# The last round of an expert loop written out, and the rounding of the next weights moved

## What is computed

```
# moe_ffn, after the router chose two experts of 16 per token
h = silu(einsum('td,edf->tef', xt, w_gate)) * einsum('td,edf->tef', xt, w_up)
h = h * comb[:, :, None]                       # gates of the chosen experts
return einsum('tef,efd->td', h, w_down)        # D = 1024, F = 512
...
# then, between the layers
x = layer_norm(DEEPNORM_ALPHA * x + ffn, ln2_g[l], ln2_b[l])
k, v = split(x @ kv_w); q = x @ w_q            # layer 1's projections
```

## Time and profile before

| | |
|---|---|
| median of 3 runs | 696.32 us (696.08 to 697.30) |
| the profiled execution | 695.99 us |
| its span, first to last instruction | 694.2 us |
| mean granted TensorE clock | 0.997 |
| PE busy | 683.0 us (98%) |
| DVE busy | 307.3 us (44%) |
| ACT busy | 229.5 us (33%) |
| POOL busy | 56.4 us (8%) |
| DMA, mean over the span | 352 GB/s |

### The profile page before, as it was taken

One profiled execution on the slowest core, in us unless ns is written; L12 is line 12 of the kernel. 1 busy time (PEld: TensorE's weight loads), 2 busy tenths in 40 slices (PEclk: granted clock), 3 DMA queues, 4 the chain that ended last, 5 costly groups with the idle time before them and its releaser, 6 DMA issues.

```text
span 694.2 us, 13450 instructions
## 1 busy us (share of the span) xinstructions
PE 683.0 (98%) x5516; PEld 408.4 (59%) x5517; DVE 307.3 (44%) x561; ACT 229.5 (33%) x432; POOL 56.4 (8%) x58
## 2 busy tenths in 40 slices
PE   9999999999999999999999999999999999999994
PEld 8989988864335335335379987887433533533531
DVE  5689956687111112112067677778711111111214
ACT  4566567152111112112173656716211111211211
POOL 2025100010000000000025000001000000000001
PEclk9999999999999999999999999999999999999998
DMA  8999334989999999999999743498999999999991
GB/s 311 311 373 397 139 121 182 406 336 423 398 422 422 419 422 419 409 422 419 415 386 390 272 157 124 180 389 343 414 414 422 421 411 422 419 406 421 421 414 68
DMA packets 51030, 244.04 MB, mean 352 GB/s; under 512 B 6233, under 2 KB 6450, under 8 KB 26418
## 3 DMA queue, kind: packets, MB, share of 16 engines
q1 hardware_dynamic: 50994, 243.55, 87.7%
HBM read 242.49 MB, written 1.05 MB: 351 GB/s over the span
## 4 chain that ended last, share of the span: by engine, by line
PE 91%; DVE 7%; issue 1%; ACT 1%; DVEq 0%; ACTq 0%
PE ps L2200 32%; PE ps L1960 11%; PE ps L1955 9%; PE ps L2214 8%; PE ps L2231 8%; PE ps L2181 5%; PE ps L2162 4%; DVE ring_lo L1214 2%; PE ps L1922 2%; PE ps L2170 1%; PE ps L1873 1%; PE ps L2128 1%; PE ps L2268 1%; PE ps L1895 1%; PE ps L1980 1%
## 5 line engine op out<-in xcount | busy, mean ns | idle before, releaser
L2200 PE MATMUL ps<-weights,scratch 128*32 128x512 f32 (+1 forms) x1536 | 167.8, 592 | 0.1
L2200 PEld LDWEIGHTS ps<-weights,scratch 128*32 128x32 f32 x1536 | 49.9, 110 | 114.0 <-issue 114.0
L1214 DVE TENSOR_TENSOR ring_lo<-weights,w_hi 128x2048 fp32r<-128x2048 f32 x35 | 83.1, 2392 | 9.2 <-ACT w_hi L818 9.0
L1730 DVE TENSOR_TENSOR scratch<-ps,early 128x512 f32<-128x512 f32 x16 | 11.0, 690 | 168.1 <-PE ps L2200 168.1
L818 ACT ACTIVATE w_hi<-weights 128x2048 fp32r<-128x2048 f32 x34 | 64.8, 1913 | 23.4 <-PE ps L1960 11.5
L1711 DVE SCALAR_TENSOR_TENSOR rounded<-ps,gslot,rounded 128x512 fp32r<-128x512 f32 x30 | 22.5, 751 | 86.3 <-ACT rounded L1080 86.3
L2200 PE MATMUL ps<-tail,scratch 128*32 128x512 f32 (+1 forms) x512 | 56.4, 592 | 0.0
L1040 ACT ACTIVATE scratch<-ps,ln_col 128x256 f32<-128x256 f32 (+1 forms) x40 | 19.4, 541 | 86.9 <-PE ps L2181 84.6
L1080 ACT ACTIVATE rounded<-ps,gslot 128x512 fp32r<-128x512 f32 x30 | 20.6, 688 | 82.9 <-PE ps L2231 41.5
L1058 ACT ACTIVATE early<-ps 128x512 f32<-128x512 f32 x16 | 9.6, 598 | 98.8 <-PE ps L2200 98.8
L2200 PEld LDWEIGHTS ps<-tail,scratch 128*32 128x32 f32 x512 | 16.6, 110 | 38.3 <-issue 38.3
(11 more groups left out here) (304 smaller groups left out, 1006.7 us busy)
## 6 DMA issues: line engine op xcount, KB each, us to landing
weights<-in_moe_w_gate SPq DMA_DIRECT2D x64, 1024.0 KB, 13.4
weights<-in_moe_w_up SPq DMA_DIRECT2D x32, 1024.0 KB, 11.7
places<-in_moe_w_down SPq DMA_DIRECT2D x32, 1024.0 KB, 11.8
tail<-in_moe_w_up SPq DMA_DIRECT2D x32, 1024.0 KB, 17.6
weights<-in_moe_w_down SPq DMA_DIRECT2D x32, 1024.0 KB, 11.8
weights<-in_a_w_in SPq DMA_DIRECT2D x15, 1024.0 KB, 12.7
weights<-in_kv_w SPq DMA_DIRECT2D x8, 1024.0 KB, 15.4
weights<-in_a_w_out SPq DMA_DIRECT2D x4, 1024.0 KB, 15.2
```

What stands on the lines that cost most here:

```text
L1214: V.tensor_tensor(low_part(i), ring[:, piece_slot(i), :, :], w_hi[:, i % HI, :, :].bitcast(F32), ALU.subtract).then_inc(lo_ready, 1)
L2200: last = mm(ps[rows, bank, :], own[:, HALF_K * part + k, rows], w, start=part == 0 and k == 0, stop=part == 1 and k == HALF_K - 1)
```

## The change

- The loop on PE runs three rounds, and the fourth is written out behind it. There `gather` has 128 moving columns, for the one pair that is left, and ACT and DVE take 128 columns out of PSUM; `add_up` is no longer behind a branch; and the odd pair's down projection goes part by part.
- ACT rounds piece 20 where it rounded piece 21, behind both evictions, and piece 21 behind its share of rounded and whole x.
- POOL no longer makes the rest of piece 20. DVE does, between the rests of the two halves of x. Piece 20 has the products in the order 0, 1, 2.
- The fill on zeros is 14 matmuls of 128 columns and 74 of 64, where there were 40 and 29.

```diff
+        def gathered_columns(two):
+            return slice(0, 2 * SLOTS if isinstance(two, int) and two == PAIRS // 2 - 1 else 4 * SLOTS)
...
                 weigh(PAIRS // 2 - 1, 1)
                 if layer == 0:
-                    i = A_PIECES
-                    pool.wait_ge(hi_ready, i + 1)
-                    pool.tensor_tensor(low_part(i), ring[:, piece_slot(i), :, :], w_hi[:, i % HI, :, :].bitcast(F32),
-                                       ALU.subtract).then_inc(lo_ready, 1)
...
-                        take_xe(xe_ps, gathered(layer, two, 0) + 1, BANK_C, (0, 1), slice(0, 4 * SLOTS))
+                        take_xe(xe_ps, gathered(layer, two, 0) + 1, BANK_C, (0, 1), gathered_columns(two))
...
                         nc.scalar.activation(rows, ps[:, bank, :], ACT.Copy, scale=gslot[:, 0:1]).then_inc(ys_act, 1)
-                        if last_pair and part == layer == 0:
-                            high(A_PIECES)
...
                 overflow()
                 if layer == 0:
-                    high(A_PIECES + 1)
+                    high(A_PIECES)
...
             rounded_and_whole(0)
             rounded_and_whole(1)
+            high(A_PIECES + 1)
...
                 V.tensor_tensor(x_lo[:, ks, :], xT[:, ks, :], x_hi[:, ks, :].bitcast(F32), ALU.subtract
                                 ).then_inc(x_lo_ready, 1)
-                if half == 1:
-                    dve.wait_ge(lo_ready, A_PIECES + 1)
-                    low(A_PIECES + 1)
+                low(A_PIECES + half)
...
-                for number in (0, 2, 1) if i == A_PIECES else range(3):
-                    w, xs = products[number]
+                for number, (w, xs) in enumerate(products):
...
-                def gather(ks, banks):
+                def gather(ks, banks, pairs=2):
+                    width = pairs * 2 * SLOTS
                     for j, k in enumerate(ks):
-                        first = (j % 2) * 4 * SLOTS
+                        first = (j % 2) * width
...
-                            last = mm(ps[:, banks[j // 2], first:first + 4 * SLOTS], part[:, t, k * P:(k + 1) * P],
-                                      pick[:, t, :, :].rearrange("p e s -> p (e s)"), start=n == 0, stop=n == 3)
+                            last = mm(ps[:, banks[j // 2], first:first + width], part[:, t, k * P:(k + 1) * P],
+                                      pick[:, t, 0:4 * pairs, :].rearrange("p e s -> p (e s)"), start=n == 0, stop=n == 3)
...
-                def experts(two, odd):
+                def experts(two, odd, last_pairs=False):
+                    pairs = 1 if last_pairs else 2
...
                     if odd:
                         add_up(1)
+                    elif last_pairs:
+                        add_up(0)
+                        add_up(1)
                     else:
                         with pe.If(two > 0):
...
-                    if odd:
+                    if odd and last_pairs:
+                        pe.wait_ge(ht_ready, pair + 1)
+                        out_of_hidden(two, odd, 0, who)
+                        out_of_hidden(two, odd, 1, who)
+                    elif odd:
                         pe.wait_ge(ht_ready, pair + 1)
                         out_by_banks(two, odd, who)
...
-                with pe.Fori(0, PAIRS // 2, 1) as two:
+                with pe.Fori(0, PAIRS // 2 - 1, 1) as two:
                     experts(two, 0)
                     experts(two, 1)
+                experts(PAIRS // 2 - 1, 0, last_pairs=True)
+                experts(PAIRS // 2 - 1, 1, last_pairs=True)
...
-            for _ in range(40):
+            for _ in range(14):
                 nothing(BANK_A, COLS // 4)
-            for _ in range(29):
+            for _ in range(74):
                 mm(ps[:, BANK_A, 0:SLOTS], zeros16[:, :], zeros16[:, 0:SLOTS], start=True, stop=True)
```

More of the change, by code:

```diff
@@ L1066, in experts @@
                     if not odd:
-                        take_xe(xe_ps, gathered(layer, two, 0) + 2, BANK_B, (4, 5), slice(0, 4 * SLOTS))
+                        take_xe(xe_ps, gathered(layer, two, 0) + 2, BANK_B, (4, 5), gathered_columns(two))
                     act.wait_ge(put_ps, pair + 2)
@@ L1732, in experts @@
                     if not odd:
-                        take_xe(gathered(layer, two, 0) + 1, (2, 3), slice(0, 4 * SLOTS))
+                        take_xe(gathered(layer, two, 0) + 1, (2, 3), gathered_columns(two))
                     if not odd:
-                        take_xe(gathered(layer, two, 0) + 2, (6, 7), slice(0, 4 * SLOTS))
+                        take_xe(gathered(layer, two, 0) + 2, (6, 7), gathered_columns(two))
                     dve.wait_ge(gslot_ready, pair + 1)
@@ L2260, in experts @@
                         pe.wait_ge(xr_ready, 2 * layer + 2)
-                        gather(range(0, 4), (BANK_C, BANK_D)).then_inc(xe_ps, 1)
+                        gather(range(0, 4), (BANK_C, BANK_D), pairs).then_inc(xe_ps, 1)
                     if odd:
@@ L2277, in experts @@
                     if not odd:
-                        gather(range(4, 6), (BANK_B,))
+                        gather(range(4, 6), (BANK_B,), pairs)
                         pe.wait_ge(xe_dve, gathered(layer, two, 0) + 1)
-                        gather(range(6, 8), (BANK_D,)).then_inc(xe_ps, 1)
+                        gather(range(6, 8), (BANK_D,), pairs).then_inc(xe_ps, 1)
                         pe.wait_ge(ht_ready, pair + 1)
```

## The result

| | before | changed |
|---|---|---|
| median in the same job | 696.07 us (695.84 to 697.30, 6 runs) | 700.06 us (698.82 to 700.74, 6 runs) |
| profiled execution | 695.99 us | 700.42 us |
| span | 694.2 us | 698.5 us |
| mean granted TensorE clock | 0.997 | 0.995 |

The ratio is 1.0054, with a 95% interval of 1.0044 to 1.0064: the change makes the kernel slower by about 4 us, outside the predicted range, and I had given slower a chance of 0.14. Of the six executions two kept a mean granted clock of 0.997 and took 698.82 and 699.22 us; the other four, at 0.993 to 0.995, took 699.99 to 700.74.

What follows compares the result with a forecast made beforehand. The prediction took PE, busy for 98% of the span, as the bound; gather's -0.5 us and the moved rounding's +0.5 summed to 0.0 on 695.99, a median of 696.3 us, with a range of 694.8 to 697.9.

Steps and rivals of the forecast that it cites:

- Step 2: Narrower evictions on ACT and DVE, the branch around add_up and the loop's end: nobody waits, so 0.
- Step 6: The fill: 2.9 us in place of 3.1, either ending before DVE's x is there, so 0.
- the third rival: The thin fill lets TensorE's clock fall before pieces 20 and 21: 2.2 us, 698.5 us; chance 0.05.
- Step 1: Gather's 64 narrow matmuls in the last rounds: step from 0.119 to 0.112 us, limited by weight loads, -0.5 us.
- both ends of the bound: Gather's narrow step as low as 0.056 us, like bf16 (-4.0 us), or 0.22, like true float32 (+6.6 us).
- Step 3: Last down chunks part by part: eviction margin 0.08 us, cost 0; late chunk's margin of 0.25 us widens, gain 0.
- Step 4: ACT's rounding of pieces 20 and 21 between the layers: done before PE reaches piece 21, so 0.
- Step 5: Rest of piece 20 moved from POOL to DVE: two PE waits, 0.27 and 0.24 us, together +0.5 us, in layer 0.

Runs made afterwards that it cites:

- Run 10: Kernel before with the last round written out in both layers and its gather at 128 columns, nothing else changed: 700.35 us, ratio 1.0054.
- run 9: Changed kernel with TensorE's jumped-over overflow code left out for layer 0: 695.98 us, ratio 0.9993 to the kernel before.
- run 2: Kernel before with only the new thin fill, 14 matmuls of 128 columns and 74 of 64: 696.62 us, ratio 1.0007.
- run 1: Changed kernel with the fill of before, 40 matmuls of 128 columns and 29 of 64: 698.63 us, ratio 1.0037 to the kernel before.
- run 11: Kernel before with the last round written out and gather at 128 columns in layer 1 alone, down projection bank by bank: 696.29 us, ratio 0.9999.
- run 12: Kernel before with layer 1's last round alone written out, narrow gather, and its odd pair's down projection part by part: 695.85 us, ratio 0.9999.
- run 7: Kernel before with only the moved rounding on ACT, DVE and POOL and piece 20's order 0, 1, 2: 697.75 us, ratio 1.0012.
- run 5: Changed kernel with a never-taken branch of 64 matmuls at the start of PE's program: 700.83 us, in two groups; ratio 1.0057 to the kernel before.

## Why the prediction was wrong

- **Step 2 failed:** "the cover is the work that PE has already queued." It put leaving the loop at 0, and a gap of 2.81 us was there. The instruction queue carried no packet between 192 and 352 us before, and four in the changed kernel: the loop's rounds run on code that is at hand, a written-out round brings its own. With it the block boundary and the jump over the overflow code fell so that 54 matmuls were left when PE needed the next block. Run 10 shows that the written-out round is enough for the gap, and run 9 that the gap goes with the overflow code; how the jump and the place of the boundary share in it stays open. I looked for the gap at the start of the written-out round; it came behind its end, where the matmuls are shortest.
- **Step 6 failed with it:** "Either ends before DVE's x is there at 357.79, so 0." True where instructions are there (runs 2 and 9). In the change the time from the fill's start to the transposes grew by 2.95 us. I compared lengths, and did not ask whether a shorter matmul uses up code faster: 54 matmuls cover 1.95 us with the new fill, 2.64 with the old one (run 1).
- **The clock** did fall, as the third rival said, and cost 1.09 us on the transposes and some 0.7 on the fill, which the 2.95 contain. But it fell behind the gap, not because of the thin fill: run 2 has the thin fill, no gap and no loss of clock. It need not fall: behind the gap of run 10 it stayed up.
- **Step 1 was right.** 16 narrow steps take 1.74 us, 0.109 each, where I took 0.112; both ends of the bound, -4.0 and +6.6, are out. Two layers gain 0.17 x 4 = 0.7 us in the groups, 0.3 per layer over the whole stretch.
- **Step 3 was right in cost, too small in worth.** C's rest ended before PE read it, and no wait stood there. But the margin of 0.25 us was not enough once `gather` was quicker: run 11 has the wait of 0.78 us, run 12 does not. In run 11 PE came to the chunk some 0.3 us earlier than before, and the chunk landed at 677.24, 0.6 us later than before; why it took longer, 18.4 us where it took 17.4, is not shown. I gave the order no gain since nothing waited; with the round written out something would.
- **Step 4 was right:** no wait for ACT's rounded weights stands in piece 20 or 21.
- **Step 5 was right in kind, short in size.** The waits for the rest of x and of the weights came, 0.29 and 0.28 us for the 0.27 and 0.24 forecast; a third distance grew by 0.10. In all +0.67 in run 7, +0.43 in the change itself.

Without the gap, then, the sum is -0.6 + 0.67, near nothing, and run 9, at 0.9993 of the kernel before, agrees with that. The forecast failed on the one term that had a sentence and no price.

## What to carry to other kernels

A round taken out of a hardware loop is new code that has to be fetched while it runs; where a skipped branch and a row of very short matmuls follow, ask how much work PE has in hand when the next 16 KB are due, and look at the instruction queue and at "issue" waits before and after. Such a gap can cost twice, since the clock can fall behind it. And a saving ahead of a late transfer is only worth what the transfer's margin leaves, so the order that widens the margin belongs to the saving.

## What the runs showed of the hardware

- PE stood still for 0.8 to 5.0 us for want of instructions; around the gap of the changed kernel the DMA engines moved 386 to 391 GB/s.
- Code that is never run sets the time: 64 matmuls in a branch that is not taken made the changed kernel 3.4 us slower in the median (703.47 against 700.06, of two jobs).
- The rounds of the loop ran without a packet of code (none from 192 to 352 us before), while the stretch with one round written out took four of 16 KB. By that, and as an estimate, PE keeps more than two such blocks at hand.
- What makes the chip ask for a block was not settled: the packet came at about the same time with and without the jump (run 9), and run 5 varies by 7 us from one execution to the next.
- A float32r matmul with new 128x128 weights has a step of 0.109 us with 128 columns (1.74 / 16) and 0.119 with 256 (1.91 / 16).
